# A hybrid gMLP and band-attention layer on one core: turning the probabilities in 64-query halves, first in a step, with VectorE copying one of two banks

## The reference

```
scores = einsum('bnqhd,bnkhd->bnhqk', qc, kb) * HEAD_DIM_B**-0.5 + bias
scores = where(valid, scores, -inf)
p = softmax(scores, axis=-1)
o = einsum('bnhqk,bnkhd->bnqhd', p, vb)
out = layernorm(ALPHA * x + concat(A * silu(z_A), B * silu(z_B)) @ w_out)
```

## Time and profile before

| | |
|---|---|
| median of 3 executions | 1104.69 us (1104.37 to 1105.38) |
| profiled execution, its own time | 1103.96 us |
| its span in the profile | 1101.9 us |
| mean granted TensorE clock | 0.999 of full speed (2.4 GHz) |
| TensorE busy | 1080.6 us (98%), 6760 matmuls |
| VectorE busy | 467.7 us (42%) |
| ScalarE busy | 329.7 us (30%) |
| GpSimd busy | 213.2 us (19%) |
| transposes of probabilities (L1275) | 560, from 640.6 to 1061.4 us |
| sums (L1312) | 1120 instructions |

### The profile page before, as it was taken

One profiled execution on the slowest core, in us unless ns is written; L12 is line 12 of the kernel. 1 busy time (PEld: TensorE's weight loads), 2 busy tenths in 40 slices (PEclk: granted clock), 3 DMA queues, 4 the chain that ended last, 5 costly groups with the idle time before them and its releaser, 6 DMA issues.

```text
span 1101.9 us, 16630 instructions
## 1 busy us (share of the span) xinstructions
PE 1080.6 (98%) x6760; PEld 925.9 (84%) x6760; DVE 467.7 (42%) x964; ACT 329.7 (30%) x692; POOL 213.2 (19%) x163
## 2 busy tenths in 40 slices
PE   7999999999999999999999999999999999999997
PEld 5988889999999999999998877777887777888875
DVE  6535441211212112111121034677676676667655
ACT  6410101111111112111121134454544445454430
POOL 0111112011010000000000001354433334443331
PEclk9999999999999999999999999999999999999999
DMA  9561114221211423333421455674455454344322
GB/s 343 182 179 47 39 39 131 84 71 65 72 55 60 142 105 129 106 122 115 141 90 51 127 178 180 170 251 141 145 165 164 130 156 135 115 142 125 124 84 80
DMA packets 129963, 137.28 MB, mean 125 GB/s; under 512 B 7496, under 2 KB 103904, under 8 KB 129888
## 3 DMA queue, kind: packets, MB, share of 16 engines
q1 hardware_dynamic: 124992, 121.54, 35.0%
q10 hardware_dynamic: 4896, 14.68, 4.1%
HBM read 86.62 MB, written 52.72 MB: 126 GB/s over the span
## 4 chain that ended last, share of the span: by engine, by line
PE 95%; DVE 2%; DMA 2%; ACT 1%; issue 1%; POOLq 0%; DVEq 0%; POOL 0%; ACTq 0%; SPq 0%
PE s_ps L1165 34%; PE s_ps L1182 16%; PE out_ps L1335 15%; PE pt_ps L1165 8%; PE pt_ps L1275 6%; PE o_ps L1312 6%; PE s_ps L1243 5%; PE s_ps L1335 2%; DVE prob L1053 1%; DMA big_raw<-w_all 1%; PE o_ps L1194 1%; PE out_ps L1194 1%; DMA bias<-s_skew 1%; PE s_ps L1205 1%; ACT prob L875 0%
## 5 line engine op out<-in xcount | busy, mean ns | idle before, releaser
L1165 PE MATMUL s_ps<-xh,ring 128*128 128x512 f32 (+1 forms) x1200 | 341.2, 362 | 0.8 <-ACT st L840 0.8
L1165 PEld LDWEIGHTS s_ps<-xh,ring 128*128 128x128 f32 x1200 | 221.2, 188 | 24.5 <-issue 1.2
L1165 PE MATMUL s_ps<-xl,ring 128*128 128x512 f32 (+1 forms) x600 | 217.1, 362 | 0.0
L1182 PE MATMUL s_ps<-ring,xh 128*128 128x512 f32 x544 | 170.7, 395 | 0.0
L867 ACT ACTIVATE pt<-pt_ps 128x512 f32<-128x512 f32 (+1 forms) x168 | 82.3, 525 | 180.3 <-PE pt_ps L1275 180.3
L1165 PEld LDWEIGHTS s_ps<-xl,ring 128*128 128x128 f32 x600 | 112.6, 188 | 11.9
L1182 PEld LDWEIGHTS s_ps<-ring,xh 128*128 128x128 f32 x544 | 99.8, 188 | 19.2
L1182 PE MATMUL s_ps<-ring,xl 128*128 128x512 f32 x272 | 106.1, 390 | 0.0
L1034 DVE CUSTOM_DVE_ANT_1 prob<-s_ps,bias 128x640 f32<-128x640 f32 (+1 forms) x112 | 85.6, 801 | 47.5 <-PE s_ps L1243 47.2
L1335 PE MATMUL out_ps<-wo_h,yh 128*128 128x512 f32 x248 | 102.1, 412 | 0.0
L875 ACT ACTIVATE prob<-prob,low 128x640 f32<-128x640 f32 (+3 forms) x136 | 100.5, 745 | 4.1 <-DVE low L1034 4.1
(11 more groups left out here) (130 smaller groups left out, 1223.0 us busy)
## 6 DMA issues: line engine op xcount, KB each, us to landing
raw<-w_all ACTq DMA_DIRECT2D x26, 512.0 KB, 3.7
yr<-s_y SPq DMA_DIRECT2D x17, 512.0 KB, 5.0
r<-x SPq DMA_DIRECT2D x17, 512.0 KB, 3.7
q<-s_q SPq DMA_DIRECT2D x16, 512.0 KB, 4.1
k<-s_k SPq DMA_DIRECT2D x16, 512.0 KB, 5.3
y_out<-r SPq DMA_DIRECT2D x15, 512.0 KB, 2.8
s_y<-st SPq DMA_DIRECT2D x24, 256.0 KB, 2.4
x_raw<-x_t SPq DMA_DIRECT2D x12, 384.0 KB, 13.3
```

Source lines behind the costliest of these rows:

```text
L1165: last = nc.tensor.matmul(bank[b][:, 0:width], w[:, kc, :], xx[:, kc, :], start=kc == 0 and a == 0, stop=kc == KC - 1 and a == 2)
L1182: last = nc.tensor.matmul(out, xx[:, kc, cols], ring[:, 0:GRP, side, kc, :], start=kc == 0 and a == 0, stop=kc == KC - 1 and a == 2)
```

## The change

The transposes of a pair unit are made in halves: 64 queries (rows) of the probabilities against a 64 x 64 piece of the identity, 64 columns moving, the first 64 queries into one PSUM bank and the second 64 into the other. The first eight blocks (four key tiles, two heads) come as one group, the two blocks of the fifth key tile as a second one. In TensorE's step the first group stands ahead of the scores, the second right behind them, ahead of the output matmuls. The second group uses the same places of the banks, and so waits for both copies of the first. The sums of all five key tiles follow in one go at the end of the step. VectorE copies the bank of the second 64 queries of the first group, as the first thing of its step; ScalarE copies the other bank, and then both halves of the fifth key tile, both ahead of its exponents. Stream units keep their two transposes of 128 rows, which now also stand ahead of the scores.

```diff
-def turned_groups(u):
+def turned_copies(u):
     kind, t, _ = UNITS[u]
-    return -(-2 * key_tiles(t) // 4) if kind == "pair" else 2
+    return 1 + (key_tiles(t) > 4) if kind == "pair" else 2
...
-        pt_ps = [ctx.enter_context(nc.psum_tensor(f"pt_ps{e}", [P, 4, P], f32)) for e in range(2)]
+        pt_both = ctx.enter_context(nc.psum_tensor("pt_ps", [P, 2, 8, HD], f32))
...
             def copy_turned(unit, e):
...
-                    m = min(4, 2 * key_tiles(t) - 4 * e)
-                    nc.scalar.activation(pt[unit % 2][:, 4 * e:4 * e + m, :], pt_ps[group % 2][:, 0:m, :],
-                                         ACT.Copy).then_inc(pt_copied, 1)
+                    held = pt[unit % 2][:, 8:10, :].rearrange("p g (h t) -> p h g t", h=2)
+                    nc.scalar.activation(held, pt_both[:, :, 0:2, :], ACT.Copy).then_inc(pt_copied, 1)
...
-                for e in range(min(2, groups)):
+                for e in range(turned_copies(step - 1) if 1 <= step <= NU else 0):
                     copy_turned(step - 1, e)
                 if step in SPLIT:
                     y_high_part(SPLIT.index(step))
                 if step < NU:
                     for h in range(heads_of(step)):
                         exponent(step, h)
-                if groups > 2:
-                    copy_turned(step - 1, 2)
...
+            def copy_turned_half(unit):
+                _, t, _ = UNITS[unit]
+                m = min(8, 2 * key_tiles(t))
+                dve.wait_ge(turned, 2 * COPIES_BEFORE[unit] + 2)
+                if unit == 1:
+                    dve.wait_ge(ya_full, GRP * NCH)
+                nc.vector.tensor_copy(pt[unit % 2][:, 0:m, HD:P], pt_both[:, 1, 0:m, :]).then_inc(pt_half_copied, 1)
+
             for step in range(STEPS):
+                if 1 <= step <= NU and UNITS[step - 1][0] == "pair":
+                    copy_turned_half(step - 1)
...
             def turn(unit, e):
-                if group >= 2:
-                    pe.wait_ge(pt_copied, group - 1)
-                elif group == 0:
+                if unit == 0:
                     pe.wait_ge(evac[4], BANK_USED[4])
+                else:
+                    pe.wait_ge(pt_copied, COPIES_BEFORE[unit] + e)
+                    pe.wait_ge(pt_half_copied, PAIRS_BEFORE[unit] + e)
...
-                for i in range(4 * e, min(4 * e + 4, 2 * key_tiles(t))):
-                    b, h = i // 2, i % 2
-                    last = nc.tensor.transpose(pt_ps[group % 2][:, i - 4 * e, :],
-                                               prob[slot(unit, h)][:, lo + b * P:lo + (b + 1) * P], ident[:])
-                last.then_inc(turned, 1)
+                lo, blocks = P if t == 2 else 0, min(8, 2 * key_tiles(t) - 8 * e)
+                for i in range(blocks):
+                    b, h = (8 * e + i) // 2, i % 2
+                    for half in range(2):
+                        rows = slice(HD * half, HD * half + HD)
+                        last = nc.tensor.transpose(pt_both[:, half, i, :], prob[slot(unit, h)][rows, lo + b * P:lo + (b + 1) * P],
+                                                   ident[rows, rows])
+                        if i == blocks - 1:
+                            last.then_inc(turned, 1)
...
             for step in range(STEPS):
+                if 1 <= step <= NU:
+                    turn(step - 1, 0)
                 if step < NU:
                     if UNITS[step][0] == "stream":
                         stream_scores(step)
                     else:
                         scores(step)
-                groups = turned_groups(step - 1) if 1 <= step <= NU else 0
-                for e in range(min(2, groups)):
-                    turn(step - 1, e)
+                if 1 <= step <= NU and UNITS[step - 1][0] == "pair" and turned_copies(step - 1) > 1:
+                    turn(step - 1, 1)
                 if 2 <= step < NU + 2 and UNITS[step - 2][0] == "stream":
                     turn_back(UNITS[step - 2][1])
                 quarter(step)
-                if groups > 2:
-                    turn(step - 1, 2)
                 if 1 <= step <= NU:
                     weigh(step - 1)
```

More of the change, by code:

```diff
@@ L166 @@
 HEADS_BEFORE = before(heads_of)
-GROUPS_BEFORE = before(turned_groups)
+COPIES_BEFORE = before(turned_copies)
+PAIRS_BEFORE = before(lambda u: UNITS[u][0] == "pair")
 STREAMS_BEFORE = before(lambda u: UNITS[u][0] == "stream")
@@ L376, in hybrid_stream_step @@
         pt_copied = sem("pt_copied")
+        pt_half_copied = sem("pt_half_copied")
         weighed = sem("weighed")
@@ L857, in copy_turned @@
                 kind, t, _ = UNITS[unit]
-                group = GROUPS_BEFORE[unit] + e
-                act.wait_ge(turned, group + 1)
+                act.wait_ge(turned, 2 * COPIES_BEFORE[unit] + (2 * e + 2 if kind == "pair" else 4))
                 if unit == 1 and e == 0:
@@ L863, in copy_turned @@
                     rows = PAST if e == 0 else SN
[L864 to L868 removed]
+                    src = pt_both[0:rows, e].rearrange("p g t -> p (g t)")[:, 0:P]
+                    nc.scalar.activation(pt[unit % 2][0:rows, e, :], src, ACT.Copy).then_inc(pt_copied, 1)
+                elif e == 0:
+                    m = min(8, 2 * key_tiles(t))
+                    nc.scalar.activation(pt[unit % 2][:, 0:m, 0:HD], pt_both[:, 0, 0:m, :], ACT.Copy).then_inc(pt_copied, 1)
+                else:
+                    held = pt[unit % 2][:, 8:10, :].rearrange("p g (h t) -> p h g t", h=2)
+                    nc.scalar.activation(held, pt_both[:, :, 0:2, :], ACT.Copy).then_inc(pt_copied, 1)
             def exponent(unit, h):
@@ L1260, in turn @@
                 kind, t, _ = UNITS[unit]
-                group = GROUPS_BEFORE[unit] + e
                 pe.wait_ge(normed, HEADS_BEFORE[unit + 1])
-                if group >= 2:
-                    pe.wait_ge(pt_copied, group - 1)
-                elif group == 0:
+                if unit == 0:
                     pe.wait_ge(evac[4], BANK_USED[4])
+                else:
+                    pe.wait_ge(pt_copied, COPIES_BEFORE[unit] + e)
+                    pe.wait_ge(pt_half_copied, PAIRS_BEFORE[unit] + e)
                 if kind == "stream":
-                    held = prob[slot(unit, 0)][:, 0:PAST] if e == 0 else prob[slot(unit, 0)][:, PAST:SKEYS]
-                    rows = PAST if e == 0 else SN
-                    nc.tensor.transpose(pt_ps[group % 2][0:rows, 0, :], held, ident[:]).then_inc(turned, 1)
+                    past, new = (pt_both[:, half].rearrange("p g t -> p (g t)")[:, 0:P] for half in range(2))
+                    nc.tensor.transpose(past, prob[slot(unit, 0)][:, 0:PAST], ident[:]).then_inc(turned, 2)
+                    nc.tensor.transpose(new[0:SN], prob[slot(unit, 0)][:, PAST:SKEYS], ident[:]).then_inc(turned, 2)
                     return
-                lo = P if t == 2 else 0
-                for i in range(4 * e, min(4 * e + 4, 2 * key_tiles(t))):
-                    b, h = i // 2, i % 2
-                    last = nc.tensor.transpose(pt_ps[group % 2][:, i - 4 * e, :],
-                                               prob[slot(unit, h)][:, lo + b * P:lo + (b + 1) * P], ident[:])
-                last.then_inc(turned, 1)
+                lo, blocks = P if t == 2 else 0, min(8, 2 * key_tiles(t) - 8 * e)
[7 more added lines that the diff above has]
+                            last.then_inc(turned, 1)
             def sums_free(unit):
@@ L1291, in weigh @@
                 kind, t, p = UNITS[unit]
-                pe.wait_ge(pt_copied, GROUPS_BEFORE[unit] + min(2, turned_groups(unit)))
+                pe.wait_ge(pt_copied, COPIES_BEFORE[unit] + (1 if kind == "pair" else 2))
+                if kind == "pair":
+                    pe.wait_ge(pt_half_copied, PAIRS_BEFORE[unit] + 1)
                 sums_free(unit)
```

6 lines of the change are left out of this document (3 added, 3 removed).

## The result

The changed kernel takes **1118.97 us** (median of 4 runs, 1117.79 to 1121.21), the kernel before beside it 1105.04 us: ratio 1.0133, 95% interval 1.012 to 1.0145. The forecast was 1110 us and slower; the time lies in the range of 1095 to 1122, but above the forecast case's own 1105 to 1116, and the loss is 14 us where 5 were forecast. The profiled execution is the longest of the four: 1121.21 us, of which 1119.2 are the span.

What follows compares the result with a forecast made beforehand. TensorE, busy 98% of the span, was taken as the bound. Shorter steps (-12.1) and fewer key tiles (-3.0) against late copies, streams and weight splits summed to +5.9 us: about 1110 us, range 1095 to 1122.

Steps and rivals of the forecast that it cites:

- the forecast case: Whole kernel: the summed terms give about 1110 us, own range 1105 to 1116, chance 0.5.
- Halves side by side, 0.057 a pair: TensorE's turnings: two row halves run at once, 0.057 us a pair against 0.109, 0.52 us out for ten turnings.
- one behind the other: Rival, TensorE's turnings: row halves run in sequence, 0.114 us a pair, +27 us, 1131 us; chance 0.1.
- Half copy 0.67: VectorE's PSUM copy of 512 elements takes 0.67 us, releasing the fifth tile 1.53 us after the first turning load.
- held by GpSimd: Rival, VectorE's half copy: GpSimd delays it once in four steps, about 3.5 us x 14, 1159 us; chance 0.02.
- Late by 0.68 behind the fourth step: Fourth step of an output tile: half copy queues behind residual and moments, TensorE idles 0.68 us; nine steps, +6.1 us.
- Up to step 20: The kernel's steps up to 20: the forecast's terms laid on them make about +3.2 us.
- Weight splits 3.5 and 2.2: At 690 and 724 us: normalises wait for GpSimd, no longer covered by computed scores; +3.5 and +2.2 us.
- Steps 20 to 57: The stretch with the stream steps: the forecast's terms laid on it make some +3.6 us.
- Steps 57 to 71: The stretch after the stream steps: the forecast's terms laid on it make -1.5 us.
- The last step: Final step: no scores cover a late copy, +0.4 us.
- TensorE alone sets the time: Rival, whole kernel: copies and residuals never hold TensorE, -23.5 us, so 1081 us; chance 0.1.

Runs made afterwards that it cites:

- keep_busy: The changed kernel with idle matmuls, which nothing reads, put into five long waits of TensorE (steps 13, 20, 40, 45, 72): 1114.72 us.
- old_order: The changed kernel's half turnings in the order of the kernel before, ScalarE copying both banks in one instruction, VectorE none: 1091.13 us, ratio 0.9878.
- stats_later_pool_short: The changed kernel with VectorE's statistics and moments behind the next step's bias, GpSimd's gain and offset cut to one column: 1102.18 us.
- pool_short_after: The changed kernel with GpSimd's gain and offset on one column instead of 1024, all waits and signals kept: 1115.08 us, ratio 1.009.
- pool_short_before: The kernel before with GpSimd's gain and offset on one column instead of 1024, all waits and signals kept: 1103.01 us, ratio 0.9987.
- order_alone: The kernel before, whole turnings, with only the order changed and all ScalarE copies ahead of its exponents: 1128.92 us, ratio 1.0221.

## Why the prediction was right in direction and short in size

The step that failed is a missing term: **no step of the sum asked what TensorE's clock does after a wait**. The sum priced each wait at its own length. The runs showed that waits are often followed by a stretch at 1.2 GHz that costs another 1.6 us, five times in the profiled execution. keep_busy measured the term: 4.2 us of the 9 by which the forecast missed. Of the other 4.7, 1.2 lie behind the last step, which the sum left as it was, and the rest are, on balance, waits between steps 20 and 57 that were sized too small. Point by point (the shares of the forecast are its terms, laid on the steps to which their conditions belong; the measured ones are of the profiled execution):

- **Halves side by side, 0.057 a pair: right.** Sixteen take 0.64 us in the chain with their first load (0.49 in old_order, 0.061 a pair), and with the fifth tile's wait, changes and loads an ordinary step is 6.04 against the forecast 6.02. The rival "one behind the other" is out; old_order turns it into 13 us.
- **Half copy 0.67: right.** The group of this line has a median of 691 ns and no instance above 692, also beside GpSimd's offset at 901.13. The rival "held by GpSimd" did not occur.
- **Late by 0.68 behind the fourth step: right.** From the last score's start to the fifth tile's first turning 0.90 us pass there (997.11 to 998.01) and 0.24 in an ordinary step (1009.91 to 1010.15): 0.66 more. That the cause is VectorE's queue ahead of the copy is shown by the chain above and by stats_later_pool_short.
- **Up to step 20: right in the number, in part by luck.** Forecast about +3.2, measured +2.8. But 1.6 of that is the clock, which was not forecast, so the waits came out 2 us smaller.
- **Weight splits 3.5 and 2.2: the sum near, neither part right.** Beside old_order steps 12 to 14 lost 3.2 us, 1.6 of them clock, and steps 17 to 20 lost 3.3: 1.6 of waiting against 3.5, and 3.3 against 2.2.
- **Steps 20 to 57: wrong.** Forecast some +3.6, measured +12.9. Three stretches at half clock are an estimated 4.8 of that; some 4.5 remain. The distances of the table, taken step by step in both traces, show where. Steps 37 and 57 lost 1.9 us more than forecast, step 45 lost 1.5, steps 28, 32, 48 and 52 together 1.9, steps 35 and 55 together 0.7, step 22 another 0.6; others lost less than forecast. Two of these have a cause in the rows. Ahead of steps 37 and 57, in VectorE's steps 36 and 56, the first of their four, the second normalise meets GpSimd's first operation, which the forecast had not counted:

```profile
842.90 3.79 POOL L738 TENSOR_SCALAR r<-r,mv_o,rstd_o 128x1024 f32<-128x1024 f32 x1
...
845.69 1.35 DVE L1056 TENSOR_SCALAR prob<-prob,rden 128x640 f32<-128x640 f32 x1
```

  And the placing of a stream's operands meets GpSimd at step 45; it was counted at 0.7 and not as held. The timeline of VectorE in front of the wait of 1.7 us at 899.5, and GpSimd beside it:

```profile
897.61 1.06 DVE L1073 COPY kt<-ks 128x64 f32<-128x64 f32 x1
897.71 0.99 DVE L1074 COPY qd<-qs 64x64 f32<-64x64 f32 x1
898.73 2.37 DVE L1075 COPY qd<-qs 64x64 f32<-64x64 f32 x1
901.13 0.69 DVE L1128 COPY pt<-pt_ps 128x512 f32<-128x512 f32 x1
```

```profile
894.84 3.79 POOL L738 TENSOR_SCALAR r<-r,mv_o,rstd_o 128x1024 f32<-128x1024 f32 x1
898.71 2.34 POOL L741 TENSOR_TENSOR r<-r,gain 128x1024 f32<-128x1024 f32 x1
```

  Three copies that have a median of 0.19 us each take 1.06, 0.99 and 2.37 here, and the last ends with GpSimd's gain. pool_short_after confirms both: without the long gain step 45 loses 0.2 us and not 1.5 beside pool_short_before, while the normalise before step 37, next to an operation that was not cut, still takes 1.34 us. In all, the meetings with gain and offset were not sized too small: the forecast gave them 3.3 us, and the two pool_short runs put them at 2.6. The smaller losses, at the first steps of four and at steps 22, 35 and 55, have no cause of their own shown.
- **Steps 57 to 71: right.** Forecast -1.5, measured -2.3 us.
- **The last step: too small.** Forecast +0.4, measured +2.8: a gap of 1.8 and the clock behind it.
- **Behind the last step: missing.** Forecast nothing, measured +1.2, and its cause stays open.
- **The rival "TensorE alone sets the time", 1081 us:** not here, but old_order comes within 10 us of it with the same matmuls. It was right in what it said of TensorE and wrong in that this order allows it.

What the change as a whole did: the halves are a gain of 13 us, the order a loss of 28. The fifth tile ahead of the output matmuls is 15.8 of the loss, the first turnings ahead of the scores 11, VectorE's half copy 1.1. Neither place buys anything, since an ordinary step takes 6.05 us either way. That the order alone loses without the halves too (24.6 us) shows that it isn't their combination.

## What to carry to other kernels

Look at what stands between a producer on another engine and the matmul that needs it: in this kernel the same twelve output matmuls a step were worth 16 us of span when they lay over a copy, and nothing when they lay behind it. Price a wait of TensorE not at its length alone, but ask whether the clock falls behind it. And before moving a small operation on VectorE, follow what it starts on GpSimd and what that will lie over: the late statistics lost 30 us with GpSimd's two operations in the way, and gained 13 without them.

## What was not expected of the hardware

- Gaps of TensorE of 1.7 to 2.2 us, and once two of 0.84 and 1.0, were followed by stretches at a granted clock of 0.50 in a kernel that is 96% busy, five times in the changed kernel's trace; with matmuls that nothing reads in five long waits it stayed at 1.00. Other gaps as long were not followed by one, and what tells them apart stays open.
- Beside GpSimd's TENSOR_TENSOR on 1024 elements (2.34 to 2.49 us) VectorE's normalise of 640 elements took up to 2.44 us in place of 0.55, and a copy of 64 elements within SBUF 2.37 in place of 0.19. Beside its TENSOR_SCALAR (L738, 3.79 us) most took their usual time. Those that were held in the changed kernel's trace started within the last 1.01 us of it: two normalises, at 845.69 and 976.06, of 1.35 and 1.24 us, which ended 0.35 behind it, and three copies, at 771.72, 897.61 and 897.71, of 1.02, 1.06 and 0.99 us, which ended 0.05 to 0.08 behind it. Normalises and copies that started 1.07 us or more ahead of its end were not held. VectorE's copy out of PSUM was never slower than 692 ns, in 64 instances.
- With whole turnings a fourth change of shape in a step cost 0.15 us, by our reading of order_alone's rows (0.37 us against 0.22 for the same two turnings), where the forecast took 0.1 for one.
